# Modulation totals summed by single-column matmuls instead of rows, a copy and transposes

## The chip, the cores and the metric

The kernel runs on one NeuronCore of a Trainium2 chip. The metric is the device time of one execution in microseconds (us); lower is better. Engines: PE multiplies matrices, DVE (VectorE) and ACT (ScalarE) do elementwise work, POOL (GpSimd) a little of it, SP issues most DMAs. On-chip tensors have 128 partitions.

## The reference

A block of two layers (a convolution mixer, a mixer with a linear recurrence and dilated attention, two gated feed-forward nets) is followed by two layers of a second kind, with adaptive modulation. In the second kind, each of 18 vectors of 1024 numbers (9 a layer: shift, scale and gate for three sublayers) comes from one product of a vector with a matrix:

```python
c_act = jax.nn.silu(c)                       # c: (1, 1024)
for l in range(2):
    mod = c_act @ ada_w[l] + ada_b[l]        # ada_w[l]: (1024, 9216)
    (sh1, sc1, g1, sh2, sc2, g2, sh3, sc3, g3) = jnp.split(mod, 9, axis=-1)
    h = modulate(rms_norm(x, ffn1_norm[l]), sh1, sc1)      # h * (1 + scale) + shift
    x = x + 0.5 * g1 * swiglu(h, w_gate1, w_up1, w_down1)
    h = modulate(rms_norm(x, mix_norm[l]), sh2, sc2)
    ...                                      # pooling and latent attention, times g2
    h = modulate(rms_norm(x, ffn2_norm[l]), sh3, sc3)
    x = x + 0.5 * g3 * swiglu(h, w_gate2, w_up2, w_down2)
```

The sequence has 256 positions, the width is 1024, the inner width of the feed-forward nets 2816, and everything is float32.

## The kernel before, in words

**Layout.** Activations lie with channels on partitions: X is [128, 8, 256], channel t*128+p at partition p, block t. A scale or shift per channel is therefore a column per block: MOD holds the 18 vectors as 18 x 8 columns and starts with the bias ada_b.

**Weights.** All weight matrices pass in "units" of up to 128 x 2048 numbers: SP loads a unit into one of three raw buffers (L466), ACT rounds it to its high half wh (`hi`, L1087), DVE makes the low half wl (`lo`, L1514), PE uses both (`w_used`). The order of the units is fixed; each engine's program is written out by hand, in order, and waits on counters. hi(n) waits until unit n-3 has been used; the load of unit n waits until unit n-3 is split.

**The modulation vectors.** The matrix ada_w is not sent through PE. While the feed-forward nets ffn0, ffn1, fa0, fb0 and fa1 run, DVE (`ada_step`, L1613) multiplies blocks of 128 of its rows by the matching column of c_act and adds them up: a total [128, 1024] per vector, in the free part of Z. What is left is the sum of each total over the partitions. It is done in five places, `ADA_GAP`: od (4 vectors, in the recurrent mixer's input projection), fa0 (3, at the start of the first modulated net), w0 (4, in the projections of the modulated mixer), fa1 (3) and w1 (4).

**The sum before.** `ada_sum_rows` (PE, L694) takes a column of ones, placed by the constant `pick` so that vector v lands in output row v, as weights (4 columns) and moves the totals, 512 columns at a time, in two halves: 2n float32 matmuls for n vectors, into two PSUM banks as rows. `ada_take` (ACT, L1107) copies the 4 x 1024 rows into AR. `ada_turn` (PE, L706) transposes them, 8 blocks of 4 x 128, into 32 columns of a bank. `ada_read` (DVE, L1522) adds these to MOD and counts `ada_out`. Other code then makes gains and shifts from MOD (`gain_cols`, `half_cols`, `shift_cols`).

**Where these steps stand.** In od, the sums come after unit 3 of od_in, the transposes after unit 5, the reading after the recurrence. In a net fa0 or fa1 the sums come first, before the net's first unit; PE waits for ACT's copy (`between`) before the norm's statistic; the transposes come before the last down unit, and the reading is in DVE's `at_end`. In w0 and w1 the sums come after the statistics of the latent norms, in bank 2 and 3, before the two q_b units; ACT's copy is before its copies of q; the transposes stand after the rotary products (L1029 to L1031) and before the value products; the reading is behind DVE's rotary step (L2101 to L2108). DVE's order in that stage is: reciprocal and latent norms (L2072), their low half (L2075), `lo(n0+7)` (w_kv_b), four shifted sums of the pooling (L2084) and an edge (L2088), `lo(n0+8)`, the pooling's differences (L2093), `lo(n0+9)`, the rotary step, and then the masks of the attention.

Of the kernel before, what the change touches and what calls it, by code (L numbers as in the profile page):

```python
# [24 lines left out]
P = 128  # L25
D = 1024
# [83 lines left out]
def const_layout():  # L110
    at = 0
    for name, n in (("ident", P), ("ones", P), ("freq", 1), ("eps", 1), ("mask", 3 * P), ("identb", P // 2), ("heads", 22), ("rot", P),
                    ("cmask", 2 * P), ("krdup", P), ("krrot", P), ("pick", 7), ("edge", 4 * 16)):
        CONST[name] = (at, n)
        at += n
    return at
# [7 lines left out]
def constants():  # L124
    import numpy as np
    c = np.zeros((P, NCONST + NSEL), np.float32)

    def put(name, v):
        a, n = CONST[name]
        c[:v.shape[0], a:a + n] = v.reshape(v.shape[0], n)  # L130

    put("ident", np.eye(P, dtype=np.float32))
    q = np.arange(P)[:, None]
    k = np.arange(2 * P)[None, :]
    steps = P + q - k
    m = np.zeros((P, 3, 2 * P), np.float32)
    for g, (window, dil) in enumerate(((128, 1), (512, 4), (2048, 16))):
        ok = (steps >= 0) & (steps <= window) & (steps % dil == 0)
        m[:, g] = np.where(ok, 0.0, -1e30)

    def halves(v):
        bits = np.ascontiguousarray(v.astype(np.float32)).view(np.uint32) >> 16
        return (bits[:, 0::2] | bits[:, 1::2] << 16).astype(np.uint32).view(np.float32)

    put("mask", halves(m.reshape(P, 3 * 2 * P)))
    put("identb", halves(np.eye(P)))
    put("cmask", np.where(steps >= 0, 0.0, -1e30).astype(np.float32))
    put("ones", np.ones((P, P), np.float32))
    h = np.zeros((P, 22), np.float32)
    h[:64, 10] = h[64:, 11] = 1.0 / 64  # L150
    for i in range(12):
        c[i, NCONST + 64 * i:NCONST + 64 * (i + 1)] = 1.0
    put("heads", h)
    r = np.zeros((64, 64), np.float32)
    for i in range(32):
        r[i + 32, i] = -1.0
        r[i, i + 32] = 1.0
    rr = np.zeros((P, P), np.float32)
    rr[:64, :64] = rr[64:, 64:] = r
    put("rot", rr)  # L160
    put("krdup", np.concatenate([np.eye(64), np.eye(64)], 1).astype(np.float32))
    put("krrot", np.concatenate([r, r], 1))
    e = np.zeros((P, 4, 16), np.float32)
    for g in range(4):
        w = 2 ** (g + 1)
        e[:, g] = (w / np.minimum(np.arange(16) + 1, w)).astype(np.float32)
    put("edge", e)
    inv = (np.float32(1.0) / np.power(np.float32(10000.0), np.arange(0, 64, 2, dtype=np.float32) / np.float32(64))).astype(np.float32)
    put("freq", np.tile(inv, 4)[:, None])
    pk = np.zeros((P, 7), np.float32)  # L170
    pk[:, 3] = 1.0
    put("pick", pk)
    put("eps", np.full((P, 1), EPS, np.float32))
    return c
# [93 lines left out]
def build(nc, A, const, out):  # L268

    ctx = ExitStack()  # L270
    with ctx:
# [3 lines left out]
        def sem(name):  # L275
            return ctx.enter_context(nc.semaphore(name))
# [38 lines left out]
        def bank(i, a=0, n=512, rows=slice(0, P)):  # L315
            return PS[rows, i, a:a + n]
# [37 lines left out]
        ada_out = sem("ada_out")  # L354
        ada_rows, ada_taken = sem("ada_rows"), sem("ada_taken")
        aux_in = [sem(f"aux_in{i}") for i in range(3)]
# [255 lines left out]
        def _(pe):  # L612
# [80 lines left out]

            def ada_sum_rows(name, bk):  # L694

                n, at = ADA_GAP[name], AC_AT[ADA_FROM[name]]
                if ADA[name]:
                    pe.wait_ge(ada_out, ADA[name])
                pe.wait_ge(ada_sum, KD * (ADA[name] + n))
                for h in range(2):  # L700
                    for v in range(n):
                        last = mm(bank(bk + h, 0, 512, slice(0, 4)), lhsT=cn("pick")[:, 3 - v:7 - v],  # L702
                                  rhs=Z[:, at + v * D + 512 * h:at + v * D + 512 * h + 512], start=v == 0, stop=v == n - 1)
                last.then_inc(ada_rows, 1)

            def ada_turn(name, bk):  # L706

                pe.wait_ge(ada_taken, list(ADA_GAP).index(name) + 1)
                for t in range(KD):
                    last = pe.transpose(bank(bk, 4 * t, 4), AR[0:4, t * P:(t + 1) * P], cn("ident")[0:4, 0:4])  # L710
                last.then_inc(ada_used, 1)
# [48 lines left out]
            def ffn(f, name):  # L760
# [23 lines left out]
                if name in ADA_GAP:  # L784
                    ada_sum_rows(name, 6)

                def between():
                    if name in ADA_GAP:
                        pe.wait_ge(ada_taken, list(ADA_GAP).index(name) + 1)
                    norm(name)  # L790

                raw_unit(n0, 4, shift, first=name, between=between)
                if name == "ffn1":
# [21 lines left out]
                block(NFB - 1, 8)  # L815
                if name in ADA_GAP:
                    pe.wait_ge(g_sum, fb + NFB)
                    ada_turn(name, 4)
                down(n0 + 32, 0, NFB - 1, ends=True)
# [119 lines left out]
            for u in range(3, 13):  # L939
                pe.wait_ge(z_out, 9 + {3: 1, 4: 1, 5: 3, 6: 3}.get(u, u - 3))  # L940
                project(U0["od_in"] + u, (u - 3) % 4, fill="mix1" if u == 3 else None, token=u >= 10)
                if u == 3:
                    ada_sum_rows("od", 6)
                if u in (3, 4):
                    pe.wait_ge(aux_in[0], 16 * 16)
                    for t in (2 * u - 6, 2 * u - 5):
                        pe.wait_ge(ev("lru_xc"), t + 1)
                        if t >= 2:
# [3 lines left out]
                           stop=True).then_inc(ev("lru_gates"), 1)  # L952
                if u == 5:
                    ada_turn("od", 6)
                if 5 <= u <= 10:
# [35 lines left out]
            for l in range(2):  # L991
# [5 lines left out]
                for u in range(3, 5):  # L997
# [3 lines left out]
                    if u == 3:  # L1001
# [5 lines left out]
                        last.then_inc(ev("mq_stat"), 1)  # L1007
                ada_sum_rows(f"w{l}", 2)

                for i in range(2):  # L1010
                    w = weights(U0[f"q_b{l}"] + i, 3)
                    if i == 0:
                        pe.wait_ge(h_ready, FILL[f"cqn{l}"] + 1)
                    hq = lambda p, k: H[p][:, k, :]
                    if i == 1:
                        pe.wait_ge(ada_taken, list(ADA_GAP).index(f"w{l}") + 1)
                    for a in range(2):
                        product(bank(2 * i, a * S, S), lambda p, k: w(p, k, P * a, P), hq, 3)
                    last = product(bank(1, i * S, S), lambda p, k: w(p, k, 2 * P, P), hq, 3)
                    last.then_inc(w_used, 1)  # L1020
# [3 lines left out]
                for h in range(QH):  # L1024
# [7 lines left out]
                   stop=True).then_inc(ev("rot_full"), 1)  # L1032
                ada_turn(f"w{l}", 2)
                for b in range(NB):
# [15 lines left out]
                last.then_inc(ev("pool_full"), 1)  # L1050
                pe.wait_ge(ada_out, ADA[f"w{l}"] + ADA_GAP[f"w{l}"])
                n0, fill = U0[f"w_out{l}"], f"yw{l}"
# [18 lines left out]
        def _(act):  # L1071
# [18 lines left out]
            def raw(name, c, gain, shift=None, after=None):  # L1090
# [10 lines left out]
                for i in {0: (0,), 1: (1,), 2: (), 3: (2, 3)}[c]:  # L1101
                    A_(cols(WK, 0, KD)[:, 2 * i:2 * i + 2, :], X[:, 2 * i:2 * i + 2, :], ACT.Square).then_inc(sq_ready, 1)

            def ada_take(name, bk):

                act.wait_ge(ada_rows, list(ADA_GAP).index(name) + 1)
                A_(AR[0:4, :].rearrange("p (h c) -> p h c", h=2), PS[0:4, bk:bk + 2, :], ACT.Copy).then_inc(ada_taken, 1)  # L1107

# [219 lines left out]
            for u in range(13):  # L1328
# [11 lines left out]
                elif u < 10:  # L1340
                    i = u - 4
                    if i == 0:
                        ada_take("od", 6)
                    A_(Z[:, OD["Q"] + 512 * i:][:, 0:512], b, ACT.Copy).then_inc(ev("qk_out"), 1)
# [56 lines left out]
            for l in range(2):  # L1401
                m0 = 72 * l
                gain = lambda i: lambda t: GM[:, 3 * l + i, t:t + 1]
                for c in range(4):
                    raw(f"fa{l}", c, gain(0), 3 * l, after=U0[("ffn1", "fb0")[l]] + 33)
                ada_take(f"fa{l}", 6)
                ffn(2 + 2 * l, norm(f"fa{l}", shift=m0, deferred=U0[f"fa{l}"] + 2))
# [37 lines left out]
                nq = U0[f"q_b{l}"]  # L1445
                ada_take(f"w{l}", 2)
                act.wait_ge(w_used, nq + 1)
# [56 lines left out]
        def _(dve):  # L1504
# [28 lines left out]
            def norm(name, gain, shift=None, deferred=None, before=None):  # L1533

                v = NORMS.index(name)
                if name != "final":
                    raw_lo(name, 3, gain)
                if before is not None:
                    lo(before)
# [489 lines left out]
            for l in range(2):  # L2029
# [5 lines left out]
                def at_end():  # L2035
                    ada_read(f"fa{l}", 4)
                    dve.wait_ge(ada_out, ADA[f"fa{l}"] + ADA_GAP[f"fa{l}"])
                    gain_cols(l, 1)
                    if l:
                        half_cols(1, 0)  # L2040
                    shift_cols(l, 2 - l)
# [32 lines left out]
                dve.wait_ge(ev("mq_normed"), 5 * l + 5)  # L2074
                tt(HL[:, 0:5, :], pairs(Z[:, 0:1280]), HH[:, 0:5, :].bitcast(F32), ALU.subtract).then_inc(h_ready, 1)  # L2075
                lo(n0 + 7)

# [32 lines left out]

                ada_read(f"w{l}", 2)
                dve.wait_ge(ada_out, ADA[f"w{l}"] + ADA_GAP[f"w{l}"])
# [70 lines left out]
```

## Time and profile before

| | us |
|---|---|
| median of 3 runs | 1623.87 (1623.45 to 1624.03) |
| the profiled execution | 1621.51 |
| its span, first to last instruction | 1619.5 |
| PE busy in it | 1591.3 |
| DVE busy | 1258.6 |
| ACT busy | 855.3 |

The profile is of one execution; a line of kernel.py is written L12, and PEld is PE's loading of weights, which runs beside its matmuls. A duration in the trace runs from an instruction's start to its end; since matmuls are pipelined, the distance between starts is what one costs.

### The profile page before, as it was taken

To read this page: it belongs to the slowest core of one execution; us is meant where nothing else is said; L and a number is where in the kernel's file an instruction comes from. 1 tells how busy PE (TensorE), PEld (TensorE's weight loads), DVE (VectorE), ACT (ScalarE), POOL (GpSimd) and SP (SyncE) were. 2 spreads that over 40 slices of the span, in tenths; PEclk is the share of its full clock that TensorE was granted. 3 is DMA by queue.
4 is the path that set the end of the run, shared out by engine and by line. 5 is a ranking of instruction groups with operands and counts; after the bars stand their busy time and mean duration, and the time that the engine had idled before them with its cause. 6 is when DMAs were issued, how large, how long until landed. Compare 5 with 4: busy or idle time off the path is not lost.

```text
span 1619.5 us, 26972 instructions
## 1 busy us (share of the span) xinstructions
PE 1591.3 (98%) x11044; PEld 1451.7 (90%) x11044; DVE 1258.6 (78%) x1447; ACT 855.3 (53%) x1025; POOL 56.0 (3%) x76
## 2 busy tenths in 40 slices
PE   8999999999999999999999999999999999999998
PEld 7989899988889999899998899999899998899997
DVE  6968989886668998778878787885878887785555
ACT  5556555555455555644446464444644455564443
POOL 3001000000010000000000010000000000000000
PEclk9999999999999999999999999999999999999999
DMA  7514888654238885488874348975498854265552
GB/s 244 183 53 156 315 322 288 236 162 134 92 105 282 293 299 190 156 300 306 317 236 137 111 157 303 316 260 184 158 323 310 300 175 160 89 193 187 183 191 80
DMA packets 231439, 343.48 MB, mean 212 GB/s; under 512 B 7067, under 2 KB 194049, under 8 KB 231361
## 3 DMA queue, kind: packets, MB, share of 16 engines
q1 hardware_dynamic: 230304, 340.94, 62.1%
q0 software_dynamic: 752, 1.18, 0.2%
q8 instruction: 55, 0.90, 0.2%
q10 hardware_dynamic: 304, 0.27, 0.1%
q14 instruction: 24, 0.19, 0.0%
HBM read 341.32 MB, written 1.05 MB: 211 GB/s over the span
## 4 chain that ended last, share of the span: by engine, by line
PE 76%; DVE 11%; issue 5%; ACT 5%; SPq 1%; DMA 0%; DVEq 0%; ACTq 0%
PE PS L674 21%; PE PS L776 19%; PE PS L675 11%; PE PS L654 8%; PE PS L632 5%; DVE wl L1514 4%; PE PS L746 3%; ACT wh L1087 2%; PE PS L641 2%; PE PS L702 2%; PE PS L915 2%; DVE Z L1613 1%; PE PS L842 1%; DVE XL L1530 1%; SPq L529 1%
## 5 line engine op out<-in xcount | busy, mean ns | idle before, releaser
L1514 DVE TENSOR_TENSOR wl<-raw,wh 128x2048 fp32r<-128x2048 f32 (+2 forms) x256 | 570.1, 2230 | 156.7 <-ACT wh L1087 154.8
L674 PE MATMUL PS<-HP,wh 128*128 128x512 f32 x1728 | 607.7, 396 | 1.6 <-DVE wl L1514 1.6
L1087 ACT ACTIVATE wh<-raw 128x2048 fp32r<-128x2048 f32 (+2 forms) x256 | 475.3, 1859 | 137.2 <-PE PS L776 115.1
L675 PE MATMUL PS<-HP,wl 128*128 128x256 f32 x1728 | 483.7, 280 | 0.0
L674 PEld LDWEIGHTS PS<-HP,wh 128*128 128x128 f32 x1728 | 324.1, 188 | 76.5 <-DVE wl L1514 2.0
L776 PE MATMUL PS<-FX,wh 128*128 128x256 f32 x1920 | 344.9, 281 | 0.5 <-DVE FX L1679 0.5
L675 PEld LDWEIGHTS PS<-HP,wl 128*128 128x128 f32 x1728 | 326.2, 189 | 0.0
L776 PEld LDWEIGHTS PS<-FX,wh 128*128 128x128 f32 x1920 | 294.9, 189 | 3.1 <-issue 0.7
L776 PE MATMUL PS<-FX,wl 128*128 128x256 f32 x960 | 269.9, 281 | 0.0
L776 PEld LDWEIGHTS PS<-FX,wl 128*128 128x128 f32 x960 | 180.9, 188 | 0.0
L1613 DVE SCALAR_TENSOR_TENSOR Z<-ada,CA,Z 128x1024 f32 x126 | 161.4, 1281 | 1.3
L632 PE MATMUL PS<-FX,wh 128*128 128x258 f32 (+2 forms) x592 | 146.5, 287 | 8.6 <-ACT FX L1099 5.0
L632 PE MATMUL PS<-FX,wl 128*128 128x258 f32 (+2 forms) x592 | 144.6, 283 | 0.0
L654 PE MATMUL PS<-HP,wh 128*128 128x256 f32 x768 | 140.9, 285 | 1.2 <-ACT HP L1120 0.6
L1153 ACT ACTIVATE WK<-PS 128x512 f32<-128x512 f32 x54 | 32.4, 599 | 197.1 <-PE PS L675 197.1
L654 PEld LDWEIGHTS PS<-HP,wh 128*128 128x128 f32 x768 | 119.8, 192 | 7.3 <-issue 2.6
L632 PEld LDWEIGHTS PS<-FX,wh 128*128 128x128 f32 (+1 forms) x592 | 111.6, 189 | 13.3 <-ACT FX L1099 6.4
L632 PEld LDWEIGHTS PS<-FX,wl 128*128 128x128 f32 (+1 forms) x592 | 111.8, 189 | 0.0
L654 PE MATMUL PS<-HP,wl 128*128 128x256 f32 x384 | 107.5, 283 | 0.0
L1178 ACT ACTIVATE WK<-PS 128x512 f32<-128x512 f32 x54 | 32.1, 595 | 96.9 <-PE PS L675 96.7
L641 PE MATMUL PS<-XL,wh 128*128 128x256 f32 (+1 forms) x592 | 77.6, 283 | 0.0
L654 PEld LDWEIGHTS PS<-HP,wl 128*128 128x128 f32 x384 | 73.6, 192 | 0.0
(286 smaller groups left out, 1747.6 us busy)
## 6 DMA issues: line engine op xcount, KB each, us to landing
ada<-ada_w SPq DMA_DIRECT2D x144, 512.0 KB, 6.1
raw<-ffn_w_gate SPq DMA_DIRECT2D x66, 1024.0 KB, 5.4
raw<-ffn_w_up SPq DMA_DIRECT2D x66, 1024.0 KB, 5.5
raw<-ffn_w_down SPq DMA_DIRECT2D x66, 1024.0 KB, 5.1
raw<-od_w_in SPq DMA_DIRECT2D x13, 1024.0 KB, 5.3
raw<-ev_w_in SPq DMA_DIRECT2D x10, 1024.0 KB, 7.2
raw<-w_in SPq DMA_DIRECT2D x8, 1024.0 KB, 5.4
raw<-w_out SPq DMA_DIRECT2D x8, 1024.0 KB, 6.3
```

Source lines behind the costliest of these rows:

```text
L632: mm(bank(dst + m, 0, width, slice(0, rows[m])), lhsT=w(a, k, m * P, rows[m]), rhs=XH[:, k, 0:width], start=k == 0 and a == 0, stop=False, ...
L641: last = mm(bank(dst + m, 0, S, slice(0, rows[m])), lhsT=w(0, k, m * P, rows[m]), rhs=XL[:, k, :], start=False, stop=k == KD - 1, skip_gro ...
L654: last = mm(dst, lhsT=lhs(a, k), rhs=rhs(b, k), start=first and i == 0, stop=first and i == len(order) - 1, skip_group_check=not first)
L674: mm(pairs(bank(bk)), lhsT=lhs(0, k), rhs=HP[:, k], start=k == 0, stop=False, skip_group_check=True)
L675: last = mm(bank(bk, 0, S), lhsT=lhs(1, k), rhs=HH[:, k, :], start=False, stop=k == k_tiles - 1, skip_group_check=True)
L702: last = mm(bank(bk + h, 0, 512, slice(0, 4)), lhsT=cn("pick")[:, 3 - v:7 - v], rhs=Z[:, at + v * D + 512 * h:at + v * D + 512 * h + 512], ...
L746: last = mm(bank(bk, m * S, S), lhsT=w(a, k, m * P, P), rhs=H[b][:, k, :], start=m == 0 and k == 0 and i == 0, stop=False, skip_group_chec ...
L776: last = mm(bank(m // 2, (m % 2) * S, S), lhsT=w(a, k, m * P, P), rhs=rhs(b, k), start=begins and i == 0 and m % 2 == 0, stop=False, skip_ ...
L1087: last = A_(dst(wh), src, ACT.Copy)
L1153: A_(pairs(E), PS[:, 4:6, S:], ACT.Copy).then_inc(g_copy, 1)
L1514: last = tt(dst(wl), src, dst(wh).bitcast(F32), ALU.subtract)
L1613: ins = stt(total, w, CA[:, k:k + 1], total, ALU.mult, ALU.add)
```

## The change

The constant `pick`, the counters `ada_rows` and `ada_taken`, ACT's `ada_take` and PE's `ada_turn` are removed. `ada_cols` makes each block of 128 columns of a total the weights of one matmul, whose moving operand is a single column of ones; the result is a column, put where the transposes had put it. The reading in fa0 and fa1 moves from the end of the net to DVE's norm at its start, and in w0 and w1 from behind the rotary step to right behind L2075. PE's waits for ACT's copy become waits for `ada_out`.

```diff
-            def ada_sum_rows(name, bk):
+            def ada_cols(name, bk):
                 n, at = ADA_GAP[name], AC_AT[ADA_FROM[name]]
                 if ADA[name]:
                     pe.wait_ge(ada_out, ADA[name])
                 pe.wait_ge(ada_sum, KD * (ADA[name] + n))
-                for h in range(2):
-                    for v in range(n):
-                        last = mm(bank(bk + h, 0, 512, slice(0, 4)), lhsT=cn("pick")[:, 3 - v:7 - v],
-                                  rhs=Z[:, at + v * D + 512 * h:at + v * D + 512 * h + 512], start=v == 0, stop=v == n - 1)
-                last.then_inc(ada_rows, 1)
-
-            def ada_turn(name, bk):
-
-                pe.wait_ge(ada_taken, list(ADA_GAP).index(name) + 1)
-                for t in range(KD):
-                    last = pe.transpose(bank(bk, 4 * t, 4), AR[0:4, t * P:(t + 1) * P], cn("ident")[0:4, 0:4])
+                for v in range(n):
+                    for t in range(KD):
+                        last = mm(bank(bk, 4 * t + v, 1), lhsT=Z[:, at + v * D + t * P:at + v * D + (t + 1) * P],
+                                  rhs=cn("ones")[:, 0:1], start=True, stop=True)
                 last.then_inc(ada_used, 1)
...
             def ffn(f, name):
...
                 if name in ADA_GAP:
-                    ada_sum_rows(name, 6)
-
-                def between():
-                    if name in ADA_GAP:
-                        pe.wait_ge(ada_taken, list(ADA_GAP).index(name) + 1)
-                    norm(name)
-
-                raw_unit(n0, 4, shift, first=name, between=between)
+                    ada_cols(name, 6)
+                raw_unit(n0, 4, shift, first=name, between=lambda: norm(name))
+                if name in ADA_GAP:
+                    pe.wait_ge(ada_out, ADA[name] + ADA_GAP[name])
...
                 block(NFB - 1, 8)
-                if name in ADA_GAP:
-                    pe.wait_ge(g_sum, fb + NFB)
-                    ada_turn(name, 4)
                 down(n0 + 32, 0, NFB - 1, ends=True)
...
                 if u == 3:
-                    ada_sum_rows("od", 6)
+                    ada_cols("od", 6)
...
-                if u == 5:
-                    ada_turn("od", 6)
...
-                ada_sum_rows(f"w{l}", 2)
+                ada_cols(f"w{l}", 2)
...
                     if i == 1:
-                        pe.wait_ge(ada_taken, list(ADA_GAP).index(f"w{l}") + 1)
+                        pe.wait_ge(ada_out, ADA[f"w{l}"] + ADA_GAP[f"w{l}"])
...
                 mm(bank(0, S, S), lhsT=cn("krrot", 64), rhs=Z[0:64, ML["KX"]:ML["KX"] + S], start=True,
                    stop=True).then_inc(ev("rot_full"), 1)
-                ada_turn(f"w{l}", 2)
...
-                pe.wait_ge(ada_out, ADA[f"w{l}"] + ADA_GAP[f"w{l}"])
...
         (ACT: ada_take and its three calls removed)
         (DVE, norm)
                 if name != "final":
                     raw_lo(name, 3, gain)
+                if name in ("fa0", "fa1"):
+                    ada_read(name)
                 if before is not None:
                     lo(before)
...
                 def at_end():
-                    ada_read(f"fa{l}", 4)
                     dve.wait_ge(ada_out, ADA[f"fa{l}"] + ADA_GAP[f"fa{l}"])
...
                 tt(HL[:, 0:5, :], pairs(Z[:, 0:1280]), HH[:, 0:5, :].bitcast(F32), ALU.subtract).then_inc(h_ready, 1)
+                ada_read(f"w{l}", 2)
                 lo(n0 + 7)
...
                     last.then_inc(ev("rope"), 1)

-                ada_read(f"w{l}", 2)
                 dve.wait_ge(ada_out, ADA[f"w{l}"] + ADA_GAP[f"w{l}"])
```

## Rows read from the trace of the kernel before

**Rows 1.** The page, busy time of each engine.

```profile
PE 1591.3 (98%) x11044; PEld 1451.7 (90%) x11044; DVE 1258.6 (78%) x1447; ACT 855.3 (53%) x1025; POOL 56.0 (3%) x76
```

**Rows 2.** Waits of PE's matmuls, 880 to 930 us (total, times, longest, us).

```profile
PE PS L842 <- DVE Z L2108: 0.4, 1, 0.4
```

**Rows 3.** One line's instructions: sums (L702), transposes (L710); ns min/median/max, first and last start.

```profile
L702 PE MATMUL PS<-Z,CN x72: 592/592/592, 348.8 to 1369.7; 128*4 128x512 f32 x72
L710 PEld LDWEIGHTS PS<-CN,AR x40: 132/136/138, 370.9 to 1382.2; 4*128 4x128 f32 x40
```

**Rows 4.** Timeline of PE in w0: start, duration (us), instructions merged.

```profile
886.98 7.03 PE L702 MATMUL PS<-Z,CN 128*4 128x512 f32 x16
893.94 0.50 PE L654 MATMUL PS<-HP,wh 128*128 128x256 f32 x2
...
905.40 0.65 PE L710 MATMUL PS<-CN,AR 4*128 4x4 f32 x8
905.98 0.50 PE L654 MATMUL PS<-wh,HP 128*128 128x512 f32 x1
```

**Rows 5.** Timeline of PE at the start of fa0.

```profile
658.29 5.31 PE L702 MATMUL PS<-Z,CN 128*4 128x512 f32 x12
...
663.53 0.39 PE L632 MATMUL PS<-FX,wh 128*128 128x258 f32 x1
```

**Rows 6.** Weight loads: timeline and line of L842's; two starts of L632.

```profile
909.35 1.86 PEld L842 LDWEIGHTS PS<-Z 128*128 128x128 f32 x16 [0.77 <-DVE Z L2108]
...
L842 PEld LDWEIGHTS PS<-Z x16: 186/192/192, 909.3 to 911.0; 128*128 128x128 f32 x16
...
663.76 0.28 PE L632 MATMUL PS<-FX,wl 128*128 128x258 f32 x1
663.88 0.28 PE L632 MATMUL PS<-FX,wh 128*128 128x258 f32 x1
```

**Rows 7.** Timeline of DVE in w0; in brackets the idle time before.

```profile
889.08 1.49 DVE L2075 TENSOR_TENSOR HP<-Z,HP 128x1280 fp32r<-128x1280 f32 x1 [1.33 <-ACT HP L1437]
890.88 2.29 DVE L1514 TENSOR_TENSOR wl<-raw,wh 128x2048 fp32r<-128x2048 f32 x1 [0.31 <-ACT wh L1087]
893.09 1.28 DVE L2084 TENSOR_TENSOR WK<-Z 128x1084 f32<-128x1084 f32 x1
...
896.65 0.44 DVE L2088 TENSOR_TENSOR WK<-WK,CN 128x16 f32<-128x16 f32 x4
899.90 2.29 DVE L1514 TENSOR_TENSOR wl<-raw,wh 128x2048 fp32r<-128x2048 f32 x1 [2.81 <-ACT wh L1087]
902.11 1.43 DVE L2093 SCALAR_TENSOR_TENSOR WK<-WK,Z 128x256 f32<-128x256 f32 x4
903.63 2.29 DVE L1514 TENSOR_TENSOR wl<-raw,wh 128x2048 fp32r<-128x2048 f32 x1
905.84 0.68 DVE L2101 TENSOR_TENSOR WK<-PS,SIN 128x512 f32<-128x512 f32 x1
...
908.43 0.86 DVE L2108 TENSOR_TENSOR Z<-WK 64x256 f32<-64x256 f32 x2
```

**Rows 8.** Timeline of ACT in w0.

```profile
894.05 1.02 ACT L1107 ACTIVATE AR<-PS 4x1024 f32<-4x1024 f32 x1 [3.20 <-PE PS L702]
...
897.96 1.90 ACT L1087 ACTIVATE wh<-raw 128x2048 fp32r<-128x2048 f32 x1
...
901.68 1.92 ACT L1087 ACTIVATE wh<-raw 128x2048 fp32r<-128x2048 f32 x1
```

**Rows 9.** Timeline of DVE at the start of fa0.

```profile
661.87 2.28 DVE L1514 TENSOR_TENSOR wl<-raw,wh 128x2048 fp32r<-128x2048 f32 x1
666.49 2.29 DVE L1514 TENSOR_TENSOR wl<-raw,wh 128x2048 fp32r<-128x2048 f32 x1 [2.34 <-ACT wh L1087]
```

**Rows 10.** Stretches at the end: busy times, then granted clock, DMA share, GB/s.

```profile
1613.20:1617.50 4.30, 0.00 (x0) 0.00 (x0) 2.54 (x8) 2.83 (x8) 0.00 (x0) 1.00 0.40 146
1617.50:1618.00 0.50, 0.00 (x0) 0.00 (x0) 0.00 (x0) 0.00 (x0) 0.00 (x0) 0.81 1.02 385
```

More of the change, by code:

```diff
@@ L112, in const_layout @@
     for name, n in (("ident", P), ("ones", P), ("freq", 1), ("eps", 1), ("mask", 3 * P), ("identb", P // 2), ("heads", 22), ("rot", P),
-                    ("cmask", 2 * P), ("krdup", P), ("krrot", P), ("pick", 7), ("edge", 4 * 16)):
+                    ("cmask", 2 * P), ("krdup", P), ("krrot", P), ("edge", 4 * 16)):
         CONST[name] = (at, n)
@@ L169, in constants @@
     put("freq", np.tile(inv, 4)[:, None])
-    pk = np.zeros((P, 7), np.float32)
-    pk[:, 3] = 1.0
-    put("pick", pk)
     put("eps", np.full((P, 1), EPS, np.float32))
@@ L354, in build @@
         ada_out = sem("ada_out")
-        ada_rows, ada_taken = sem("ada_rows"), sem("ada_taken")
         aux_in = [sem(f"aux_in{i}") for i in range(3)]
@@ L1102, in raw @@
                     A_(cols(WK, 0, KD)[:, 2 * i:2 * i + 2, :], X[:, 2 * i:2 * i + 2, :], ACT.Square).then_inc(sq_ready, 1)
-            def ada_take(name, bk):
-                act.wait_ge(ada_rows, list(ADA_GAP).index(name) + 1)
-                A_(AR[0:4, :].rearrange("p (h c) -> p h c", h=2), PS[0:4, bk:bk + 2, :], ACT.Copy).then_inc(ada_taken, 1)
             def norm(name, shift=None, deferred=None):
@@ L1341, in _ @@
                     i = u - 4
-                    if i == 0:
-                        ada_take("od", 6)
                     A_(Z[:, OD["Q"] + 512 * i:][:, 0:512], b, ACT.Copy).then_inc(ev("qk_out"), 1)
@@ L1405, in _ @@
                     raw(f"fa{l}", c, gain(0), 3 * l, after=U0[("ffn1", "fb0")[l]] + 33)
-                ada_take(f"fa{l}", 6)
                 ffn(2 + 2 * l, norm(f"fa{l}", shift=m0, deferred=U0[f"fa{l}"] + 2))
@@ L1445, in _ @@
                 nq = U0[f"q_b{l}"]
-                ada_take(f"w{l}", 2)
                 act.wait_ge(w_used, nq + 1)
```

## The prediction

> **What bounds the kernel now.** I read the page's table of engines first: PE is busy for 1591.3 of 1619.5 us [rows 1]. Then the waits of PE around the ten places that the diff touches: near the fa0 sums and beside the od sums there are none, and in the w0 stage PE stands still once at the rotary step, 0.4 us before the first scores (L842), for DVE [rows 2]. So what counts is how long PE is occupied by the old and the new sums, and at w0 and w1 how long DVE takes from the sums to L2108. I then took the old sums and transposes (rows 3 to 5), the nearest weight loads (rows 6), and DVE's and ACT's order in the w0 stage (rows 7, 8). w1 repeats w0 and fa1 repeats fa0 to within 0.03 us, so one of each is shown.
>
> **What goes from PE.** The sums over partitions are 36 float32 matmuls of 4 weight columns and 512 moving ones, each with two records: 72 records [rows 3], in five bursts. A burst with four vectors (od, w0, w1) has 16 records and holds PE from 886.98 to 893.94: 6.96 us, 0.429 a record with 0.1 at the end [rows 4]. One with three (fa0, fa1) has 12 and takes 663.53 - 658.29 = 5.24 us [rows 5]. The eight transposes of each place take 905.98 - 905.40 = 0.58 us [rows 4]. So four vectors cost 7.54 us of PE, three cost 5.82, and all five places 3 x 7.54 + 2 x 5.82 = 34.3 us.
>
> **What comes to PE.** Each vector has 8 blocks of 128 columns; each block becomes the weights of a float32 matmul with one moving column: 18 x 8 = 144 matmuls, 288 records if each has two as now. Nothing in the trace is such a record; call its spacing c. The moving column is next to nothing, so the weight load must set it. From below: the transposes load 128 columns too and move only 4; their loads last 136 ns each [rows 3], yet they are spaced 0.58 / 8 = 72 ns or, without the 0.1 us at the end, 61 [rows 4]. That shows that loads overlap even when almost nothing moves. But such a load is of a shorter kind; a float32 load of 128 columns for a real product lasts 192 ns [rows 6]. Nearest: the 16 records of the first scores, same type, same 128 weight columns: their loads end 1.86 us after the first began, so (1.86 - 0.19) / 15 = 0.111 us each [rows 6]. Next above: the rounded units of L632 at 0.12 us [rows 6], with 258 moving columns. From above: no overlap at all, 0.192 or more. I take 0.113, by the scores' row, a little up because DVE and ACT read memory beside it. Four vectors: 64 x 0.113 + 0.1 = 7.33 us, three: 48 x 0.113 + 0.1 = 5.52.
>
> The Trainium skill, "TensorE: Matmul & The Clock Gate", Part 3 (What overlaps and what doesn't), says that a weight load runs beside matmuls in flight only where the row groups differ, and here all 128 rows are used. By that c would be the full load of 192 ns (rival 1). The scores' row speaks against it: loads of 192 ns with the same rows stand 111 ns apart.
>
> **Place by place, c = 0.113.**
> - od: 7.33 - 7.54 = -0.2 us. PE is the bound on both sides of it. DVE reads the result only after the recurrence, and ACT's copy of the rows (1.02 us, rows 8 has its twin) was beside PE; it goes for nothing. POOL's load behind ada_used is issued some 6 us earlier, behind its own earlier load; nobody waits for it.
> - fa0 and fa1: 5.52 - 5.82 = -0.3 us each, -0.6 together. The 0.58 us of the transposes before the last down unit lie on PE's path. ACT loses its copy, so it splits unit n0+2 about 3 us earlier, which nobody needs. DVE gets the reading (0.2 us) in the middle of norm, with a wait for the last sum: that ends at 658.29 + 47 x 0.113 + 0.3 = 663.9, where DVE would have started the low half of unit n0+1 at 661.87 [rows 9]. That split ends 2.2 us later, at 666.4, and PE needs it only after about 16 + 10 + 16 more records, past 671; the next split, which was waiting for ACT until 666.49 [rows 9], now starts at 666.3. Behind it stands the reciprocal, which waits for the root near 670. So the wait is covered, by 3 us. SP's load of unit n0+4 goes out 2.2 us later and is split more than 10 us after that. The wait added on PE (ada_out) is long met.
> - w0 and w1, PE: 7.33 - 6.96 = +0.37 at the sums, -0.58 at the transposes, which stand right before the value products. PE would be ready for the first scores 0.2 us earlier than now (909.0, the 0.4 us of [rows 2] before they start).
> - w0 and w1, DVE: this is where the change costs. The reading moves from behind the rotary step (0.22 us, in front of DVE work that then waits for scores anyway: worth nothing) to right behind L2075. L2075 ends at 890.57 [rows 7], before half of the sums are done. The last one starts at 886.98 + 63 x 0.113 = 894.10 and is seen by DVE 0.3 us later, 894.4. DVE stands 3.6 us, with everything behind it: three splits, the pooling sums, the rotary step. Before, the idle time in that line was 0.31 us (at 890.88) and 2.81 us before 899.90, where L1514 waits for ACT; that slack is eaten. Forward from 894.4: reading 0.22, split 2.21 (890.88 to 893.09), pooling sums 4.0 (893.09 to 897.09), which gives 900.8. ACT's half of that unit ends at 899.86 + 0.37 = 900.2 [rows 8], so DVE no longer waits for it. Then split 2.21, L2093 1.37, so the split that was at 903.63 starts at 904.4 (ACT's part is ready at 903.6 + 0.4 [rows 8]). From there to the first scores as now, 909.35 - 903.63 = 5.72 us: 910.1 in place of 909.35, +0.77. PE then stands 1.3 us instead of 0.4. What follows waits for the scores or for pool results that come after them, so it moves with them. Twice: +1.5 us.
> - Queued behind the waiting read on DVE is also the split of w_kv_b, finished at 896.8 in place of 893.1; PE wants it after two q_b units (54 records of 0.12, past 900). SP's next load comes out 3.7 us later, and its unit is split by ACT at 910. Hidden. The q_b wait on ada_out is met at 894.6; PE reaches it near 897.5.
>
> **Sum.** -0.2 - 0.6 + 1.5 = +0.7 us on the profiled execution: 1621.51 to 1622.2. With c left open the sum is 288c - 31.85 us (64c at od, 96c at fa0 and fa1, 128c in the two w stages, where DVE's start hangs on the same last sum): c = 0.107 gives -1.0, 0.120 gives +2.7. The profiled execution (span 1619.5 and 2.0 around it) is 2.36 us below the median of the runs; on the median the forecast is 1624.6 us. What a measurement can tell from no change is about 0.2%, 3.2 us.
>
> **Rivals.**
> 1. Loads and matmuls don't overlap once so little moves: c = 0.192, or above 0.122 for a slower kernel at all. Then the bursts last 12.4 and 9.3 us, and DVE in w0 and w1 waits till 899.4. 288 x 0.192 - 31.85 = +23.4: 1647. For it: no row has one moving column. Against: the transposes with four.
> 2. The clock falls. While DVE and ACT finish alone from 1613.2 on, the granted clock stays at 1.00 up to 1617.5 and is 0.81 in the next half us, on its way to 0.50, the lower level of 1.2 GHz; PE had been still since 1613.2 [rows 10]. If a burst of single columns were as good as standing still, part of it would run at half rate, and some of what follows. All five bursts at half rate from their first record would cost 3 x 7.3 + 2 x 5.5 = 33 us more, none of it 0; since the level held for 4 us of stillness there, I take the smaller half, +14: 1639. For it: the array has one column in 113 ns to compute. Against: the loads go on without a pause. The Trainium skill, same page, Part 1, says that the gate follows how busy the engine has been, and Part 4 that transposes don't count as busy in the same way; no run here shows which of these a weight load is.
> 3. Loads as dense as those of the transposes, c near 0.064: bursts of 4.2 and 3.2 us, 288 x 0.064 - 31.85 = -13.4: 1610. It is faster by over 0.2% from c below 0.099. For it: only the transposes' own spacing. Against: their load is 136 ns long, the real one 192.
> 4. The waits in w0 and w1 are hidden after all (the order on DVE costs nothing): -0.4 a place instead of +0.77, 1622.3. Against: DVE's row has only 3.1 us of idle in that line, and waits 3.6.
>
> **Chances.** Forecast with c between 0.105 and 0.122 (1622.3 to 1627.2): 0.62. Rival 1 and milder forms of it: 0.10. Rival 2: 0.09. Rival 3 and milder forms, c under 0.1: 0.11. Rival 4: 0.08. Faster by over 0.2% has rival 3 and a little of rival 4: 0.14. Slower by over 0.2% has rivals 1 and 2 and the upper edge of the forecast with whatever DVE's order costs in addition: 0.27. Within: 0.59. For eight in ten the range takes the forecast's own, rival 4 and the mild forms on both sides, and up to a third of rival 2's bound (11 us): 1619 to 1634.
>
> **What would show it.** A burst of 64 records at 7.2 to 7.4 us in w0, load 190 ns long and 113 apart; DVE idle 3.6 us before the reading behind L2075, and none before the third split; PE waiting 1.3 us for L2108 before L842; 0.58 us less before the last down unit of fa0; granted clock 1.00 at 887 to 900. A burst of more than 7.8 us, a clock below 1.00 in it, or the first scores no later than now would each prove its step wrong.

## The result: slower, and the profile after

The changed kernel takes 1643.39 us (median of 4 runs, 1642.34 to 1646.08); the kernel before, on the same chip, 1623.66 (4 runs, 1621.81 to 1624.03). The ratio is 1.0126, with a 95% interval of 1.0109 to 1.0144: slower by 1.3%, some 20 us. The forecast was 1624.6, its range 1619 to 1634. The profiled execution took 1642.69 us, with a span of 1640.9.

The page's table of engines after, against [rows 1]: PE is busy for 20.3 us more, with 174 matmul records more. So the time went into PE's work, not into waits for others. The second line is the granted clock by slices of 41 us.

```profile
PE 1611.6 (98%) x11218; PEld 1498.1 (91%) x11220; DVE 1258.2 (77%) x1447; ACT 849.9 (52%) x1020; POOL 56.4 (3%) x76
PEclk9999999989999999999999999999999998999999
```

The line of the new sums (ns min/median/max, first and last start), and who waited for it. In [rows 3] the old matmuls all took 592 ns; here load and matmul of the same shape have two durations, 187 to 192 and 338 ns for the load.

```profile
L698 PEld LDWEIGHTS PS<-CN,Z x288: 187/192/338, 349.9 to 1389.6; 128*128 128x128 f32 x144
L698 PE MATMUL PS<-CN,Z x288: 164/250/353, 350.0 to 1389.6; 128*128 128x1 f32 x144
  DVE MOD L1491: 19.0, 4
```

Why there are two is in the granted clock: windows across the bursts of od (starts 350.04) and w0 (starts 894.85). Columns: from:to, length, busy time and instructions of PE, PEld, DVE, ACT, POOL, clock, DMA share, GB/s.

```profile
350.00:352.00 2.00, 2.00 (x21) 2.00 (x19) 2.00 (x7) 2.00 (x3) 0.00 (x0) 1.00 0.44 98
352.00:354.00 2.00, 2.00 (x16) 2.00 (x16) 2.00 (x3) 1.41 (x1) 0.00 (x0) 0.76 1.08 380
354.00:366.00 12.00, 12.00 (x49) 11.28 (x50) 6.15 (x10) 1.68 (x4) 0.00 (x0) 0.50 0.60 184
366.00:368.00 2.00, 2.00 (x16) 2.00 (x15) 0.00 (x0) 0.00 (x0) 0.00 (x0) 0.82 0.00 0
...
894.00:898.00 4.00, 4.00 (x38) 4.00 (x37) 2.66 (x6) 2.85 (x3) 0.00 (x0) 1.00 0.89 283
898.00:900.00 2.00, 2.00 (x17) 2.00 (x16) 0.54 (x1) 0.81 (x1) 0.00 (x0) 0.80 0.00 1
900.00:908.00 8.00, 8.00 (x39) 8.00 (x39) 3.34 (x3) 0.00 (x0) 0.00 (x0) 0.50 0.00 1
```

Within each burst the clock falls from 1.00 to 0.50 (from 2.4 to 1.2 GHz), though PE and PEld count as busy without a gap, and it comes back only after full products have run at the low level. By the trace's clock events the five places stand at 0.50 for 13.7 (od), 3.4 (fa0), 10.2 (w0), 6.8 (fa1) and 13.7 us (w1), 47.8 in all. The bursts last 10.76, 5.53, 9.57, 6.09 and 11.54 us, from the first matmul to the first product behind them; the forecast had 7.33 and 5.52. In the kernel before, the stretches of the five old bursts and what follows them are at 1.00. The records of the burst stand 0.109 us apart at the high level (mean of 170) and 0.213 at the low one (108).

DVE in w0, against [rows 7] (start, duration, in brackets the idle time before and what ended it), then, from the waits of PE (total, times, longest), that of the first scores, against [rows 2]:

```profile
897.05 1.49 DVE L2045 TENSOR_TENSOR HP<-Z,HP 128x1280 fp32r<-128x1280 f32 x1 [1.34 <-ACT HP L1407]
904.66 0.19 DVE L1491 TENSOR_TENSOR MOD<-PS,MOD 128x32 f32<-128x32 f32 x1 [6.12 <-PE PS L698]
904.77 2.28 DVE L1483 TENSOR_TENSOR wl<-raw,wh 128x2048 fp32r<-128x2048 f32 x1
...
912.56 2.29 DVE L1483 TENSOR_TENSOR wl<-raw,wh 128x2048 fp32r<-128x2048 f32 x1 [1.60 <-ACT wh L1065]
```

```profile
PE PS L824 <- DVE Z L2079: 0.9, 1, 0.9
```

DVE stands 6.12 us for the last sum instead of the 3.6 forecast, since the burst lasts 9.57 us (894.85 to 904.42) instead of 7.3. But PE waits only 0.9 us for DVE at the first scores. They come 27.15 us behind the start of the burst in w0 and 28.80 in w1; before, 22.37 in both (909.35 - 886.98).

Where the 21.4 us between the two spans arise, from the start of one burst to the next: up to od +1.2; od to fa0 +6.0; fa0 to w0 +0.7; w0 to fa1 +4.9; fa1 to w1 +2.2; w1 to the end +6.4. The +1.2 ahead of od isn't the change's: PE has the same work up to there, and the trace after has two stretches at 0.50 of 3.4 us each (from 15.1 and 107.3) that the one before lacks.

### The profile page after: what moved, and what is told of

It reads as the page before. It is cut to its first block, busy times and chain, and to the rows that moved or that the text cites. A ratio compares the mean times of both kernels' runs of the same rounds, so it can differ in the third digit from the quotient of the medians.

```text
span 1640.9 us, 27312 instructions
## 1 busy us (share of the span) xinstructions
PE 1611.6 (98%) x11218; PEld 1498.1 (91%) x11220; DVE 1258.2 (77%) x1447; ACT 849.9 (52%) x1020; POOL 56.4 (3%) x76
## 4 chain that ended last, share of the span: by engine, by line
PE 79%; DVE 10%; issue 5%; ACT 4%; DMA 1%; DVEq 0%; ACTq 0%; SPq 0%
PE PS L670 21%; PE PS L765 19%; PE PS L671 11%; PE PS L650 9%; PE PS L628 6%; DVE wl L1483 4%; PE PS L735 3%; PE PS L637 3%; PE PS L698 3%; ACT wh L1065 2%; PE PS L897 2%; DVE Z L1584 1%; PE PS L824 1%; DVE XL L1499 1%; PE PS L710 1%
## 5 line engine op out<-in xcount | busy, mean ns | idle before, releaser
L628 PE MATMUL PS<-FX,wh 128*128 128x258 f32 (+2 forms) x592 | 150.4, 292 | 8.3 <-ACT FX L1077 5.0
L628 PE MATMUL PS<-FX,wl 128*128 128x258 f32 (+2 forms) x592 | 148.4, 288 | 0.0
L650 PE MATMUL PS<-HP,wh 128*128 128x256 f32 x768 | 146.0, 292 | 1.2 <-ACT HP L1093 0.6
L628 PEld LDWEIGHTS PS<-FX,wh 128*128 128x128 f32 (+1 forms) x592 | 114.9, 194 | 11.2 <-ACT FX L1077 6.4
```

The lines of the kernel that those rows point to most:

```text
L628: mm(bank(dst + m, 0, width, slice(0, rows[m])), lhsT=w(a, k, m * P, rows[m]), rhs=XH[:, k, 0:width], start=k == 0 and a == 0, stop=False, ...
L650: last = mm(dst, lhsT=lhs(a, k), rhs=rhs(b, k), start=first and i == 0, stop=first and i == len(order) - 1, skip_group_check=not first)
```

## The experiments

Two theories stood at the start. **Clock** (theory A in the expectations): the low clock is the cause; a matmul with one moving column leaves the array with next to nothing to do, and the chip takes that for idleness. **Structure** (B and C there): what costs is the pile of 288 weight loads and their order, or DVE's wait for the last sum in w; the clock is by the way. The lever that parts them is the number of moving columns, W: the loads and every wait stay the same. The edit also turns the order of the blocks within a burst around and lets the results overlap in the bank; W = 16 has both as well and is the control for them.

### More moving columns

```
 t outside, v inside (so that sums may overlap):
-    rhs=cn("ones")[:, 0:1]   -> bank(bk, 4 * t + v, 1)
+    rhs=cn("ones")[:, 0:W]   -> bank(bk, 4 * t + v, W)      W = 64, 128, 16
```

W = 64:

> The changed kernel with one edit: each of the 144 sums moves 64 columns of ones instead of one. The blocks are taken in the order of their places, so each matmul writes its result 64 times from its own place on and the next ones overwrite all but the first; the result is the same. Weight loads, records and waits are those of the changed kernel, and 64 moving columns (half of the 107 ns that 128 take in the scores) fit under a load of 0.109 us. Theory A (the +20 us is the clock: single-column matmuls are no work for it, it falls in each burst): the granted clock stays at 1.00 through the five bursts, a burst of 64 records takes 7.1 us, and the time is that of the forecast with the measured spacing, 288 x 0.109 - 31.85 = -0.5, so 1623 us, within 2 us of the kernel before. Theory B (the fall comes from the loads, or from the order of waits that the change made, whatever moves): the clock falls as before and the time stays at 1643. Theory C (the clock is a symptom, the time goes in DVE's wait at w0 and w1): 1640 or more.

W = 128:

> As the one with 64 columns, with 128 moving: 107 ns of moving under a load of 109 ns. Theory A: clock 1.00 in the bursts, spacing 0.111 to 0.118 us as in the first scores, 1623 to 1625 us. Theories B and C: 1640 or more.

W = 16:

> As the one with 64 columns, with 16 moving, still well under the load's 109 ns. Theory A says only that it lies between: if the array's share of busy time decides, 16 columns of 256 cycles are little and the clock falls in most bursts (1635 to 1643); if any steady stream of more than one column will do, 1623. Theory B and C: 1643.

Measured: W = 64 1622.31 us (ratio to the kernel before 0.9995, 0.9985 to 1.0004), W = 128 1622.06 (0.9994, 0.9985 to 1.0004), W = 16 1639.72 (1.0097, 1.008 to 1.0114). Three windows of W = 64 in od and w0, then two of W = 16:

```profile
348.00:352.00 4.00, 4.00 (x38) 4.00 (x37) 4.00 (x10) 4.00 (x4) 0.00 (x0) 1.00 0.60 174
352.00:356.00 4.00, 4.00 (x37) 4.00 (x37) 4.00 (x8) 0.09 (x1) 0.00 (x0) 1.00 0.57 160
885.00:893.00 8.00, 8.00 (x73) 8.00 (x72) 2.99 (x7) 3.67 (x3) 0.00 (x0) 1.00 0.38 124
```

```profile
354.00:362.00 8.00, 8.00 (x37) 7.91 (x37) 6.60 (x10) 0.00 (x0) 0.00 (x0) 0.50 0.56 170
902.00:908.00 6.00, 6.00 (x30) 6.00 (x30) 3.09 (x3) 0.00 (x0) 0.00 (x0) 0.50 0.00 1
```

Sixty-four times the moving data, and 21 us less: the kernel with W = 64 does all that the changed one does, with the same loads, and keeps 1.00. The spacing of its records is 0.1107 us, against 0.109 with one column at the same clock: behind a float32 load the columns are nearly free. W = 128 gives 0.1116. (In the kernel before, float32 matmuls of 256 and 512 moving columns last 379 and 592 ns, so 128 columns more take 107 ns: they fit beside a load.) W = 16 has the loop order and the overlapping sums of W = 64, and falls at all five places: neither order nor layout is the cause. Its median is 3.7 us below that of the kernel with one column, and this too goes with the clock: its profiled execution is the slowest of its four (1642.79 us, mean clock 0.983, 47.8 us at 0.50 in the five places, all as with one column), and the three faster ones (1637.17 to 1640.66) have a mean clock of 0.985 to 0.986. How long the low level holds varies: with one column fa0 stands 3.4 us at 0.50 in the changed kernel and 6.8 in the one with single columns in fa alone. The theory of structure is out as the main cause; what is left of it can be read from W = 64, whose clock is undisturbed: its timeline (PE in od, DVE in w0), then its waits of PE in w0.

```profile
348.72 7.26 PE L699 MATMUL PS<-CN,Z 128*128 128x64 f32 x64
355.81 0.65 PE L933 MATMUL PS<-T,PW 128*128 128x256 f32 x2
...
892.88 0.19 DVE L1492 TENSOR_TENSOR MOD<-PS,MOD 128x32 f32<-128x32 f32 x1 [3.68 <-PE PS L699]
```

```profile
PE PS L825 <- DVE Z L2080: 1.3, 1, 1.3
```

DVE's 3.68 us and PE's 1.3 us are the forecast's 3.6 and 1.3; the first scores come 22.84 us behind the burst's start, 0.47 later than before.

### One place at a time

```
-                W = 64
+                W = (1 if name in ('od',) else 64)      # or ('fa0', 'fa1')
```

One column in od alone:

> One moving column in the od burst alone, 64 in the other four. The price of a single fall of the clock: theory A (each burst pays for itself, and only through the clock) takes it from the changed kernel's trace, where the stage from the od burst to the fa0 burst took 315.5 us against 309.0 with 64 columns: +6.5 us on 1622.3, so 1628 to 1629, clock 0.50 from some 3 us into the burst to about 5 us behind it and 1.00 at the other four. A rival, that the falls feed each other (a program once slowed falls again): falls at the other bursts too, over 1632.

One column in fa0 and fa1 alone:

> One moving column in the bursts of fa0 and fa1 (48 records, 5.3 us each), 64 in od, w0 and w1. Theory A: these fall late in the burst or just behind it, 3.4 and 6.8 us at the lower level in the changed kernel's trace, so 5.1 us lost together: 1625 to 1629. If a burst of 5.3 us were short enough, 1622.3.

Measured: od alone 1628.87 us, 6.6 over W = 64 (ratio to before 1.0037, 1.0024 to 1.005); fa alone 1628.29, 6.0 over it (1.0035, 1.0022 to 1.0049). The first two windows are of the first kernel, the third is of the second:

```profile
353.00:365.00 12.00, 12.00 (x49) 11.28 (x50) 5.73 (x10) 1.68 (x4) 0.00 (x0) 0.50 0.57 175
885.00:893.00 8.00, 8.00 (x66) 7.87 (x65) 6.90 (x9) 2.58 (x6) 0.00 (x0) 1.00 0.97 347
```

```profile
664.00:670.00 6.00, 6.00 (x29) 6.00 (x29) 3.93 (x3) 1.80 (x2) 0.00 (x0) 0.50 0.08 16
```

Of the five places, the clock falls at those with single columns and at no other. The whole loss over W = 64 is 1643.39 - 1622.31 = 21.1 us (medians of different sessions, in which the kernel before had 1622.56 to 1623.66); 6.6 + 6.0 leaves 8.5 for the two w stages, which I did not run alone. The kept traces of the changed kernel and of W = 64 give each place by itself, from one burst's start to the next: od +6.5, fa0 +1.5, w0 +4.3, fa1 +3.1, w1 +6.0, together 21.3, so 10.3 for the two w stages. Each is 0.42 to 0.48 of the place's own time at 0.50 (13.7, 3.4, 10.2, 6.8, 13.7 us): near the half that work at half rate would lose.

### The single columns dispersed, and a cover taken away

Could the single columns stay, if one vector at a time stands between full units?

```
-                if u == 3:
-                    ada_cols("od", 6)
+                if 3 <= u <= 6:
+                    ada_cols("od", 6, (u - 3,))     # 16 records behind each of four units
 w: one vector behind units 3 and 4 and behind each q_b unit; fa: one ahead of the raw unit, two behind it;
 DVE reads the sums later, in fa behind the splits that follow, in w behind that of unit n0+8
```

> One moving column everywhere as in the changed kernel, but not in one burst: in od, w0 and w1 one vector (16 records, 1.75 us) after each of four units, in fa0 and fa1 one vector before the first unit and two (3.5 us) before the norm's statistic. In w0 and w1 the columns go to bank 6, and DVE reads them behind the split of unit n0+8, where nothing waits for the reading. Theory A': the clock falls only where single columns make up a long stretch without other work. Then it stays at 1.00 here and the time is that of 64 columns without DVE's waits, 1620.5 to 1622.5. Rival: single columns cost the clock wherever they stand (their share of any few us is what counts, and 1.75 in 7 us is a quarter): falls remain, above 1628.

The same places with 64 columns (the vectors' results then lie 96 columns apart in the bank, and DVE's reading follows that):

> The same places as in the spread kernel, with 64 moving columns: no fall of the clock by theory A, and no wait of DVE. PE works the same time as with 64 columns in bursts; what can be saved more is PE's wait before the first scores of w0 and w1, 1.3 us each with 64 columns in bursts and 0.9 with the late reading. If it goes to about 0.4, the time is 1.5 to 2 us under that with 64 columns: 1620.5 by medians, 0.1% under the kernel before. If the order on DVE were worth nothing: 1622.3.

Measured: 1637.76 us (1.0088, 1.0073 to 1.0104) and 1632.81 (1.0067, 1.0053 to 1.0081). Both theories failed. The first kernel is far above the 1620.5 to 1622.5 of theory A' and where its rival has it; the second was off by 12 us: with 64 columns spreading should cost nothing and cost 10.5 us over W = 64. PE in od of the second kernel shows why, by its timeline and by windows of the same stretch:

```profile
348.37 1.90 PE L699 MATMUL PS<-CN,Z 128*128 128x64 f32 x16
355.24 1.19 PE L940 MATMUL PS<-T,PW 128*128 128x256 f32 x2 [4.97 <-DVE T L1932]
```

```profile
350.00:355.00 5.00, 0.26 (x3) 0.12 (x2) 5.00 (x9) 1.74 (x1) 0.00 (x0) 0.97 0.65 207
355.00:358.00 3.00, 2.76 (x7) 2.26 (x8) 3.00 (x5) 0.62 (x2) 0.00 (x0) 0.50 0.92 317
```

Behind unit 3 of od come the gate matmuls, which need the convolution that DVE finishes at 355. The burst, old or new, had filled just this time: the gates start 6.87 us behind the start of the shortened burst (355.24 - 348.37), and 7.09 behind that of the whole one (355.81 - 348.72). With one vector there instead of four, PE stands 4.97 us, and then the clock falls too, here behind a true standstill. In w the first q_b unit waits in the same way for DVE's low half of the normed latents (HP), 1.7 us a place. Two kernels test this reading. In the first, od's burst keeps one vector of four (the sums of the other three are left out); in the second, only od of the spread kernel is put back.

```
-                    for v in range(n):
+                    for v in range(1 if name == "od" else n):
```

> The kernel with 64 ones columns, in od only vector 0 of the four is summed: 16 matmuls instead of 64 (the other three vectors' sums are left out, so the od modulation isn't the reference's). Theory (od's burst is cover: it lies in front of the first gate matmuls, which wait for the convolution on VectorE, T written by L1932 in the spread kernel, where TensorE sat idle 4.97 us in front of them): 48 x 0.109 = 5.2 us of matmuls go and about 5.0 us of idle time comes, after which the granted clock falls for one stretch; time 1622 to 1624, the 64-column kernel being 1622.3. Rival (the burst is all cost): 5.2 us less, 1617.1.

```
-                if 3 <= u <= 6:
-                    ada_cols("od", 6, (u - 3,))
+                if u == 3:
+                    ada_cols("od", 6, (0, 1, 2, 3))
```

> The spread kernel with 64 columns, with od's four vectors put back into one burst behind unit 3; fa and w stay spread. Theory (the spread kernel loses 6.1 us in od, to the wait for the convolution that the burst had covered and the clock that falls behind it; and some 2.5 us in each w, where the units of the queries now wait): 6.1 less than the spread kernel's 1632.8, so 1626.7 +-1; no wait before the gates. Rival (the loss is of the layout of the sums in the bank or of reading them later, anywhere): no change, 1632.8.

Measured: 1624.52 us (1.0011, 1.0001 to 1.002), 0.5 above what I gave and 2.2 more than W = 64 for 5.3 us of matmuls less; and 1626.58, 6.2 less than spread. PE's timeline of the first kernel, and windows of it from the end of its sums on:

```profile
350.79 1.90 PE L699 MATMUL PS<-CN,Z 128*128 128x64 f32 x16
357.65 0.77 PE L933 MATMUL PS<-T,PW 128*128 128x256 f32 x1 [4.97 <-DVE T L1925]
```

```profile
352.50:357.00 4.50, 0.19 (x2) 0.05 (x1) 4.50 (x8) 1.65 (x1) 0.00 (x0) 0.94 0.71 218
357.00:363.00 6.00, 5.34 (x17) 4.66 (x18) 3.90 (x6) 1.68 (x4) 0.00 (x0) 0.50 0.63 192
```

Both go the theory's way: all but some 0.2 us of od's burst (7.09 - 6.87) is cover, work that costs nothing because PE would otherwise wait, and taking it away brings the wait and costs the clock on top. (The Trainium skill, "TensorE: Matmul & The Clock Gate", Part 1, warns of this course: a gap in PE's work, then a restart at half clock; these windows agree, 0.94 and then 0.50.) The other 4.3 us of the spread kernel over W = 64 are in the w stages, where PE waits 1.7 us each for HP and the clock falls once each. So the time of the single spread kernel does not answer its question: in od and w the clock may have fallen by the waits, as with 64 columns. Its trace does, place by place. In fa there is no such wait, and there its 32 single records behind the unit still end at 0.50 (timeline, then a window behind them):

```profile
671.55 4.05 PE L699 MATMUL PS<-CN,Z 128*128 128x1 f32 x32
```

```profile
675.00:681.00 6.00, 6.00 (x19) 5.11 (x20) 0.56 (x2) 0.47 (x1) 0.00 (x0) 0.50 0.73 261
```

With 64 columns at the same place there is no fall (first line below). But the groups of 16 single records that stand alone between full products, without a wait of PE beside them, keep the clock: the three in od (from 366.3, 375.6 and 384.2; second line), the one ahead of the unit in fa0 and in fa1, and three each in w0 and w1. All five falls of this kernel at the sums' places are at the 32 records of fa0 and fa1 or beside a wait.

```profile
673.00:680.00 7.00, 7.00 (x53) 6.74 (x52) 4.20 (x8) 2.01 (x5) 0.00 (x0) 1.00 0.61 214
...
362.00:390.00 28.00, 28.00 (x220) 26.06 (x219) 13.53 (x5) 14.43 (x19) 1.32 (x2) 1.00 0.42 134
```

In these traces, then, single columns 16 records at a time between full products cost no clock. No kernel that spreads all of them so without uncovering a wait was run.

### DVE's wait in w

```
-                ada_read(f"w{l}", 2)
                 lo(n0 + 7)
+                ada_read(f"w{l}", 2)
```

On the changed kernel (one column):

> The changed kernel (one column), with VectorE's read of w's sums put one step later, behind the low half of unit n0+7. Theory (the low clock is most of it, VectorE's wait the small rest): the bursts stay 9 to 12 us long, the first scores come 0.3 to 1.0 us earlier in each w; 1641.5, between 1641 and 1643. Rival (VectorE's wait of 6.1 us, which stands in front of the splits, is what makes w dear): first scores 22.5 us behind the burst's start instead of 27.2 and 28.8, 11 us less in all: 1632.

On the kernel with 64 columns:

> 64 moving columns, and in w0 and w1 DVE reads the sums after the split of unit n0+7 instead of before it. Theory A plus the DVE term of the forecast (a read in front of that split makes DVE wait 3.4 us and delays the first scores by 0.5 us in each of the two stages at this spacing): 0.4 us less per stage than with 64 columns alone, 1622.3, the first scores then bound by ACT's half again. If the DVE term is wrong: the same time as with 64 columns, within 0.3 us. Theory B: 1642.

The same kernel, timed again:

> The kernel with 64 ones columns and w's sums read one step later, timed again, since its gain is close to what a measurement tells. If the gain is real: 1620 to 1621.5, ratio 0.998 to 0.9995. If its first result was the runs' scatter: 1622.3, ratio 0.9997, like the kernel with 64 columns alone.

Measured: one column 1643.01 us (1.0131, 1.0106 to 1.0156), so it gains nothing over the changed kernel (1.0126): the first scores 27.13 us behind the burst's start, PE's wait still 0.9. I had expected 0.3 to 1.0 us, and the time is at the edge of what I gave. DVE's row says where it went:

```profile
905.40 0.19 DVE L1491 TENSOR_TENSOR MOD<-PS,MOD 128x32 f32<-128x32 f32 x1 [3.37 <-PE PS L698]
...
913.45 2.29 DVE L1483 TENSOR_TENSOR wl<-raw,wh 128x2048 fp32r<-128x2048 f32 x1 [3.96 <-ACT wh L1065]
```

DVE gains 2.3 us at the reading and stands as much longer before the next split, for ACT's half. ACT in turn had idled 11.30 us for PE's unit n0+3, which runs behind the slow burst. So with one column DVE's wait is hidden behind PE's own slowness. With 64 columns it is not: 1620.62 us and, again, 1620.23 (ratio to before 0.9988, 0.9979 to 0.9998, and 0.9986, 0.9977 to 0.9995), PE's wait 0.9 instead of 1.3 us, first scores at 22.47. That is the fastest kernel of the case, about 2 us below the one before. The gain is under the 0.2% that one measurement tells, but both intervals lie below 1. Against W = 64 the medians fall by 1.7 and 2.1 us, the means by 0.8 and 1.0; the traces show 0.7 (0.37 at the first scores of each w). The interval of W = 64 (0.9985 to 1.0004) overlaps both, so more than this 0.7 isn't shown.

## Why the prediction was wrong

**The step that failed** is the assumption under the sum that all 288 records run at the high clock; the text priced the other case as rival 2, "The clock falls", at +14 us and a chance of 0.09. It is what happened: the clock stood at 0.50 for 47.8 us in the five places, and the time is +20, between that 14 and the bound of 33. Two arguments failed there. "Against: the loads go on without a pause": the page counts loads as PEld's busy time and single-column matmuls as PE's, and both were at 100% of the windows in which the clock fell. So weight loads without a pause don't keep the clock up, which the prediction had left open, and the page's busy share doesn't tell whether it will hold. And "since the level held for 4 us of stillness there, I take the smaller half" reckoned only with the burst's own records: in od the low level lasted from 353.1 to 366.7, 6 us of it behind the burst, over full products. A fall inside a burst is paid for in the work behind it as well: against W = 64 the five bursts are 11.7 us longer, and the other 9.6 of the 21.3 us come behind them.

**The spacing c**, 0.113 by the row of the first scores, was right: 0.109 at the high level. The sentence of the Trainium skill that the prediction weighed ("TensorE: Matmul & The Clock Gate", Part 3, What overlaps and what doesn't), that a weight load runs beside matmuls in flight only where the row groups differ, isn't borne out: loads that last 187 to 192 ns, all on the same 128 rows, start 0.109 us apart. The measurement decides. Rival 1 looked likely at first sight of a burst of 9.57 us (0.15 a record), but it is a mean of 0.109 and 0.213. Rival 3, as dense as the transposes, is out with W = 64.

**The other terms**, read from W = 64, where the clock is out of the way (formula with c = 0.1107: +0.0 us; measured in the spans 1618.2 - 1619.5 = -1.3):
- od: forecast -0.2, measured od to fa0 308.95 against 309.48, -0.5. The step was right, but its reason was short: "PE is the bound on both sides of it". No wait shows in front of the gates because the burst filled it. Had the burst come out at 4.2 us (rival 3), an estimated 2.7 of the 2.8 us counted as gained there (6.96 - 4.2) would have turned into this wait (6.87 - 4.2).
- fa0 and fa1: forecast -0.3 each; measured -0.8 each (fa0 to w0, fa1 to w1). The burst itself is 5.28 us against 5.24; the 0.58 of the transposes is real, and 0.3 us more is not accounted for.
- w0 and w1: forecast +0.77 at the first scores, measured +0.47. DVE's wait (3.68 us) and PE's (1.3) came as worked out. The order on DVE does cost, so rival 4 is out: the late reading takes 0.37 of it back, and even then the first scores come 0.1 later than before. (Its -0.4 a place has no working; the prediction's own terms for PE, +0.37 - 0.58 and the wait of 0.4 gone, give -0.6.)

**What would show it** said "granted clock 1.00 at 887 to 900" and "a clock below 1.00 in it"; those lines refuted the forecast at once.

**Still open:** what exactly the chip counts as activity. The runs show that loads alone don't do, that the number of moving columns matters, and that 16 single-column records between full products keep the clock where 32 or more in a row did not. The share of the two w stages is read from traces and differences (10.3 and 8.5 us), not from a run of their own.

## What to carry to other kernels

Before turning a few wide matmuls into many narrow ones, count what each new instruction moves, not how long PE looks busy. Where the weight load sets the pace, moving more columns than needed may be free (here 64 instead of 1: +0.002 us a record) and keeps the clock; the change then is worth what the arithmetic says. And a burst on the bounding engine with no wait behind it may be somebody's cover: look at what the next instruction's inputs were finished by, before counting each microsecond taken from it as gained.

## What the runs showed of the hardware

- PE and PEld busy without a gap, and yet the granted clock went from 1.00 to 0.50: with 1 or 16 moving columns behind float32 loads of 128 columns at every burst, with 64 or 128 at none.
- A float32 load of 128 columns with its small matmul takes 0.109 us of PE at 2.4 GHz and 0.213 at 1.2 GHz, although one load lasts 192 ns at the former: neighbours overlap on the same rows.
- Sixteen single-column records (1.7 us) between full products left the clock at 1.00; 32 in a row (3.9 us) ended at 0.50.
- There are short single stretches at the low level, 3.4 us each, away from all the sums: near 15, 36 or 107 us in some traces, near 475 in all but one, in the kernel before too (470.9 to 474.3). Each follows a wait of PE of 1.9 to 2.6 us (2.62 us up to 471.25 in the kernel before). The same wait near 106 us ends without a fall in other traces, so they come and go between executions and belong to none of the changes.
